# Joins of the first layer: whole-tile squares, single convolution taps, and x split tile by tile in the last output unit

## The reference

```python
# first block, l = 0 (conformer convolution), l = 1 (causal attention with forget gates)
for l in range(2):
    h = rmsnorm(x, g_mix[l])
    mem_k, mem_v = split(rmsnorm(mem, g_mem) @ w_mem_kv[l])        # mem: 256 tokens
    # l = 0: p = h @ w_in_a -> u (1536), q_mem (256)
    #        v = a * sigmoid(gate); v = causal_dwconv(v, width 31); v = silu(layernorm(v))
    x = x + concat([mix, memory_attention(q_mem, mem_k, mem_v)]) @ w_out[l]
    x = x + conv_ffn(rmsnorm(x, g_ffn[l]), ...)                    # up 2*2816, conv 3, silu*gate, down
x = rmsnorm(x, g_final)
# second block, 2 layers: rmsnorm, input projection, gated spatial mixing and GQA attention,
# output projection, x = x + rmsnorm(out, post_g)
```

## Time and profile before

| | us |
|---|---|
| median of 3 runs | 1788.6 (1787.67 to 1791.67) |
| the profiled execution, its own time | 1788.69 |
| its span | 1786.9 |
| PE busy in the span | 1685.6 (94%) |
| DVE / ACT / POOL busy | 886.1 / 739.2 / 721.1 |
| mean granted TensorE clock | 0.973 of full speed |
| DMA | 142.71 MB, mean 80 GB/s |

### The profile page before, as it was taken

One profiled execution on the slowest core, in us unless ns is written; L12 is line 12 of the kernel. 1 busy time (PEld: TensorE's weight loads), 2 busy tenths in 40 slices (PEclk: granted clock), 3 DMA queues, 4 the chain that ended last, 5 costly groups with the idle time before them and its releaser, 6 DMA issues.

```text
span 1786.9 us, 23856 instructions
## 1 busy us (share of the span) xinstructions
PE 1685.6 (94%) x8586; PEld 1292.2 (72%) x8586; DVE 886.1 (50%) x1360; ACT 739.2 (41%) x1143; POOL 721.1 (40%) x409
## 2 busy tenths in 40 slices
PE   5989899999999999999999999998999997899995
PEld 4756678888888776677788888886776676676674
DVE  7588745544420035434556666102655444655454
ACT  5333434444432245444455555222427443327350
POOL 4433343444444444443344444443334432334330
PEclk8999999999999999999999999998999998999997
DMA  5211133333333322112233333333211112211111
...
DMA packets 39819, 142.71 MB, mean 80 GB/s; under 512 B 4417, under 2 KB 4417, under 8 KB 39745
## 3 DMA queue, kind: packets, MB, share of 16 engines
...
## 4 chain that ended last, share of the span: by engine, by line
PE 82%; DVE 12%; ACT 3%; issue 2%; DMA 0%; POOL 0%; SPq 0%; DVEq 0%; ACTq 0%; POOLq 0%
PE banks L1469 23%; PE banks L1471 23%; PE banks L1470 23%; PE banks L1573 3%; PE banks L1608 3%; PE banks L1591 2%; DVE chain L1170 2%; DVE sq_sum L959 1%; PE banks L1664 1%; ACT prob L634 1%; PE banks L1541 1%; DVE pt L1456 1%; DVE xs_lo L1326 1%; PE banks L1847 1%; DVE nmax L1025 1%
## 5 line engine op out<-in xcount | busy, mean ns | idle before, releaser
L507 POOL TENSOR_TENSOR w_lo<-raw,w_hi 128x1024 fp32r<-128x1024 f32 x255 | 625.2, 2461 | 814.8 <-ACT w_hi L586 814.6
L1469 PE MATMUL banks<-xs_hi,w_hi 128*128 128x512 f32 x1592 | 649.0, 408 | 25.9 <-DVE xs_lo L1326 12.5
L1471 PE MATMUL banks<-xs_hi,w_lo 128*128 128x512 f32 x1592 | 627.3, 394 | 0.0
L1470 PE MATMUL banks<-xs_lo,w_hi 128*128 128x512 f32 x1592 | 626.7, 394 | 0.0
L586 ACT ACTIVATE w_hi<-raw 128x1024 fp32r<-128x1024 f32 x255 | 263.7, 1052 | 298.2 <-PE banks L1471 289.8
L1469 PEld LDWEIGHTS banks<-xs_hi,w_hi 128*128 128x128 f32 x1592 | 303.3, 191 | 109.3 <-issue 40.3
L1471 PEld LDWEIGHTS banks<-xs_hi,w_lo 128*128 128x128 f32 x1592 | 302.6, 190 | 65.8
L1470 PEld LDWEIGHTS banks<-xs_lo,w_hi 128*128 128x128 f32 x1592 | 303.8, 191 | 60.3 <-issue 2.9
L517 POOL TENSOR_SCALAR prob<-prob,rinv 128x512 f32<-128x512 f32 (+3 forms) x144 | 87.1, 619 | 183.6 <-DVE rinv L1034 183.5
L634 ACT ACTIVATE prob<-banks,nmax 128x512 f32<-128x512 f32 (+3 forms) x144 | 83.3, 583 | 169.6 <-DVE nmax L1025 169.4
L1471 PE MATMUL banks<-hid_hi,w_lo 128*128 128x512 f32 x352 | 139.1, 395 | 0.0
...
## 6 DMA issues: line engine op xcount, KB each, us to landing
...
out<-x SPq DMA_DIRECT2D x8, 256.0 KB, 2.0
...
sb_sb<-sbT ACTq DMA_DIRECT2D x2, 256.0 KB, 4.1
...
```

Source lines behind the costliest of these rows:

```text
L507: nc.gpsimd.tensor_tensor(w_lo[s][:].rearrange("p k c -> p (k c)"), raw[s][:], w_hi[s][:].rearrange("p k c -> p (k c)").bitcast(f32), SUB) ...
L1469: MM(dst, w_hi[slot][:, k, :], hi, start=start, stop=False)
L1470: MM(dst, w_hi[slot][:, k, :], lo, start=False, stop=False)
L1471: return MM(dst, w_lo[slot][:, k, :], hi, start=False, stop=stop)
```

## The change

It touches seven things.
1. **Start.** The squares of `memx` and x go into whole buffers `mem_sq` and `x_sq` (in the space of `glu` and `conv`, not yet used); DVE sums each with one `tensor_reduce`. ACT makes w_hi(1) behind the fourth tile of `mem_hi`, w_hi(2) before the squares of mem. The norm x has its `stat` in the second query unit and its `cast` in GLU unit 0; the two query units go to banks 2 and 3.
2. **Places.** The attention's steps move from slots 2, 7, ..., 47 to 12, 16, 21, ..., 55 (slot = 8j + k), `conv_parts` to behind units 6 to 10, `conv_fold` and `parts_down` by one unit, to 7 to 11.
3. **Taps.** DVE does one tap behind each k instead of two behind each attention step and the rest at the unit's end; `inverses` comes directly behind `maxima` and `even_down`. Of the last channel tile PE takes 24 taps and DVE 7.
4. **Layer norm.** The squares go into `glu`, no buffer has to be freed; `ln_stat` comes before the third unit of `U_MEM1`; the xs_lo of the memory tiles come behind the centring.
5. **invert.** `m` and `t` lie in the PSUM bank `b_mix`, and r alone in SBUF; no instruction has two inputs in SBUF.
6. **Last output unit.** x tiles 0 to 6 are split while PE runs unit 7 of the output projection, as it releases the tiles of xs (`xs_free`); DVE does xs_lo 0 to 5 before it adds the last unit, xs_lo 6 behind that, 7 behind the square.
7. **FFN down of layer 0.** Each tile of x is split behind its residual instead of all at the end.

```diff
-PE_TAPS = 16
-DVE_TAPS = CW - PE_TAPS
+PE_TAPS = (16, 16, 16, 16, 16, 24)
+DVE_TAPS = tuple(CW - n for n in PE_TAPS)
-A_AT = [divmod(2 + 5 * i, KT) for i in range(10)]
+A_AT = [divmod(12 + 43 * i // 9, KT) for i in range(10)]
...
-            def residual(first, name):
+            def residual(first, name, gain, change):
                 for m in range(KT):
                     high_for(first + m)
+                    if m == KT - 1:
+                        for k in range(KT - 1):
+                            tile_free(change, first + m, k)
+                            A(xs_hi[:, k, :], x[:, k, :], ACT.Copy, scale=col(gain, k)).then_inc(split_hi, 1)
                     act.wait_ge(acc_free, accs_before(first + m) + 1)
                     square(name, m, x[:, m, :])
+                A(xs_hi[:, KT - 1, :], x[:, KT - 1, :], ACT.Copy, scale=col(gain, KT - 1)).then_inc(split_hi, 1)
...
+                if k == 3:
+                    high(1)
-            high(1)
+            high(2)
             for k in range(KT):
-                if k >= 2:
-                    act.wait_ge(sq_added, norm_at["mem"][1] + k - 1)
-                A(sqm[k % 2][:], memx[:, k, :], ACT.Square).then_inc(squared, 1)
-            high(2)
+                A(mem_sq[:, k, :], memx[:, k, :], ACT.Square).then_inc(first_squared, 1)
             for k in range(KT):
                 if k % 2 == 0:
                     act.wait_ge(x_in[k // 2], 16)
                 A(xs_hi[:, k, :], x[:, k, :], ACT.Copy, scale=col("g_mix0", k)).then_inc(split_hi, 1)
-                square("x", k, x[:, k, :])
-                if k in (1, 4, 6):
-                    high(3 + (1, 4, 6).index(k))
+                A(x_sq[:, k, :], x[:, k, :], ACT.Square).then_inc(first_squared, 1)
+                if k == 1:
+                    high(3)
+            high(4)
+            high(5)
...
-                if t >= 2:
-                    act.wait_ge(ln_summed, t - 1)
-                A(sq[t % 2][:], conv[:, t, :], ACT.Square).then_inc(ln_squared, 1)
+                A(glu[:, t, 0:T], conv[:, t, :], ACT.Square).then_inc(ln_squared, 1)
...
-                m, r, t = small_m[:, 0:w], small[:, 0:w], small_t[:, 0:w]
+                m, t = (b_mix[:, TM + 64 * i:TM + 64 * i + w] for i in range(2))
+                r = small[:, 0:w]
...
-                    own.link(V.scalar_tensor_tensor(out=t, in0=r, scalar=-0.5, in1=r, op0=MUL, op1=MUL))
-                    own.link(V.tensor_tensor(t, t, m, MUL))
+                    own.link(V.tensor_tensor(t, m, r, MUL))
+                    own.link(V.scalar_tensor_tensor(out=t, in0=t, scalar=-0.5, in1=r, op0=MUL, op1=MUL))
...
-            def residual(first, name):
+            def residual(first, name, no, gain):
                 for m in range(KT):
                     u = first + m
+                    if m == KT - 1:
+                        for k in range(KT - 2):
+                            low(no, gain, k)
                     src = take_acc(u, accs_before(u))
                     V.tensor_tensor(x[:, m, :], x[:, m, :], src[:], ADD).then_inc(acc_free, 1)
+                    if m == KT - 1:
+                        low(no, gain, KT - 2)
                     add_square(name, m)
+                low(no, gain, KT - 1)
...
                     add_square(name, m)
+                    if l == 0:
+                        low(SP_Q, "g_mix1", m)
...
-                add_square("x", k)
-                if k == 3:
+                if k == 5:
                     invert("mem")
-                if k == 6:
-                    spread("mem", rstd_m, TM)
+            dve.wait_ge(first_squared, 2 * KT)
+            V.tensor_reduce(sq_sum[:], x_sq[:].rearrange("p k t -> p t k"), AX.X, ADD).then_inc(first_summed, 1)
+            spread("mem", rstd_m, TM)
...
                 for k in range(KT):
+                    at = KT * (j % 2) + k
                     for i in a_steps(j, k):
                         if i < att_m0.n:
                             maxima(att_m0, i)
-                        if t >= 0:
-                            conv_taps(t, at, at + 2)
-                            at += 2
+                        if 1 <= i <= att_m0.n:
+                            even_down(att_m0, i - 1)
                         if i < att_m0.n:
                             inverses(att_m0, i)
...
-                if t >= 0:
-                    conv_taps(t, at, DVE_TAPS if j % 2 else 8)
-                if 7 <= j < 11:
-                    conv_finish(j - 7)
+                    if t >= 0:
+                        conv_taps(t, at, at + 1)
+                if 8 <= j < 12:
+                    conv_finish(j - 8)
...
             glu_product(MT - 1)
+            own.wait()
+            conv_taps(MT - 1, 0, DVE_TAPS[MT - 1])
             conv_finish(MT - 2)
+            conv_finish(MT - 1)
+            layer_norm("ln", (0,), conv, MT, bank[2])
...
-            unit(U_QM0, U_QM0, first=KT * SP_A, before=[(2, lambda: stat("x"))], wait_acc=False)
-            unit(U_QM0 + 1, U_QM0 + 1, before=[(2, lambda: cast("x"))], wait_acc=False)
+            unit(U_QM0, U_QM0, first=KT * SP_A, wait_acc=False, dst=bank[2])
+            unit(U_QM0 + 1, U_QM0 + 1, before=[(2, lambda: stat("x"))], wait_acc=False, dst=bank[3])
...
+            ln_stat()
             mem_unit(U_MEM1 + 2, half_bank(acc[1], 0))
-            ln_stat()
+            cast("ln")
             mem_unit(U_MEM1 + 3, half_bank(acc[1], 1))
-            cast("ln")
```

152 lines of the change are left out of this document (71 added, 81 removed).

## The result

The changed kernel takes 1778.56 us (median of 4 runs, 1777.3 to 1781.08), the kernel before on the same chip 1789.74 (1787.67 to 1791.67): ratio 0.9938, 95% interval 0.9927 to 0.995, so 11.2 us faster. The forecast was 1767.0 and its range ended at 1778: the direction was right, half of the gain was missing, and the time lies just outside the range.

What follows compares the result with a forecast made beforehand. PE, busy 94% of the span, was taken to bound the kernel, with some 100 us idle at joins and DVE pacing the GLU stretch. From 1788.69, -4.0 - 5.4 - 0.4 - 4.6 - 1.1 - 6.2 = -21.7 gave 1767 us; range 1754 to 1778.

Steps and rivals of the forecast that it cites:

- Start: From the kernel's beginning to GLU unit 0: that unit begins at 43.5 instead of 55.8, 12.3 us earlier.
- My lower bound for the gain, 9: At the start: gain of only 9 us if the transfers or ACT hold up w_hi(2) and w_hi(4).
- GLU stage: GLU units, paced by DVE: product 0 to product 2 takes 48 to 49 us; only 4 of 12.3 + 2.5 arrive.
- Last tile and layer norm: Last convolution tile through layer norm to the projection's first tile: -3.9 - 0.6 - 0.9 = -5.4 us.
- net -0.6: Layer norm: statistics start at once, the next unit covers the inversion, PE idles 1.4 us before the first square; net -0.6.
- Last output units: Last output-projection unit, twice: PE's wait moves from the FFN's first tile to `stat`; gain 0.2 us each.
- Down stage: FFN down stage of layer 0: the 2.93 us wait and 1.7 of low clock go, -4.6 us.
- Inversion: Norm inversions: no instruction waits for POOL; -1.1 us in f1 and -6.2 in pre0 and pre1 together.
- The bound of 3.6 for writing PSUM: Inversion: at worst 0.1 us more per instruction, 1.2 in each of three exposed inversions, 3.6 in all; nothing was taken.
- The third rival: GLU stage eats the start's whole gain; unit 11 ends where it did or 3 us later, 1771 to 1775; chance 0.13.
- the forecast's own test of being wrong: Wrong if GLU unit 11 ends before 163 or after 173, or if `stat` of f0 is not waited for.

Runs made afterwards that it cites:

- b4: The changed kernel with the high split of weight unit 1 put behind all eight of memory's splits on ACT; 1779.08 us, ratio 0.9926.
- c3: The changed kernel with DVE's taps 2 to 5 of the convolution left out in tiles 0 to 4; 1771.14 us, ratio 0.9905.
- d2: c1 with PE doing 20 of the taps in tiles 0 to 2 instead of 16; 1764.78 us, ratio 0.9854.
- b3: The changed kernel with the order around the layer norm as in the kernel before; 1772.32 us, ratio 0.9897.
- d4: c1 with a tap put back between maxima and inverses, and b4's edit; 1761.94 us, ratio 0.9842.
- c1: The changed kernel with the edits of a3 and b3 together; 1764.1 us, ratio 0.9864.
- a3: The changed kernel with the next weights' high split on ACT put behind the last output unit's splits of x; 1768.49 us, ratio 0.9879.
- a2: The kernel before with only x split tile by tile in the FFN down stage of layer 0; 1783.78 us, ratio 0.9967.
- a1: The kernel before with only the inversion's m and t moved into the PSUM bank; 1780.79 us, ratio 0.9954.

## Why the forecast was right, and where it was wrong

The sum said -21.7 and the profile shows -7.6. In the order of the forecast's steps:

- **Start: mis-sized, 4.1 us.** (The forecast's own terms, 29.5 + 10.9 + 0.9 + 1.7, add up to 43.0 and not to 43.5, so by its working 4.6.) "The two reduces of DVE (I take 2.1 and 4.3 us, at the rate of its other instructions) lie beside PE" is the step that failed. They took 3.83 and 7.50, the longer ends at 40.8 and not near 31, and `stat` of x waits 2.35 us for it. The low clock behind it (3.4 us of it, 1.7 lost) is no more than the forecast had counted. Two things had to come together for the wait: the sum is 3.2 longer, and it begins at 33.37 instead of near 27, since VectorE's splits and the inversion of mem stand before it (the last two `xs_lo`, beside `w_lo`, take 3.70). Either by itself would have fitted before 38. The other 2 us lie ahead of that: the first query unit begins at 31.49 and not at 29.5, as ScalarE makes its `w_hi` from 27.94 on and not by 27.0, and PE waits 1.17 for GpSimd's part. One of them is of this execution: PE's first matmul comes at 10.00, in the kernel before at 8.98 and in most kernels below between 8.7 and 9.2. The strided sum of one input costs 1.83 ns per element (7.50 us for 4096), where an operation over 512 elements costs 0.69 us, 1.35 ns. My lower bound for the gain, 9, left this out. Beside it, the early split of weight unit 1 makes GpSimd hold `mem_lo` (four took 5.59); b4 prices that at 1.0.
- **GLU stage: the mechanism right, 2.3 short.** From product 0 to product 2 I said 48 to 49 us, and it is 48.6; that VectorE's taps bind there is shown by c3, with d2's exception. (12.3 and 2.5 off 73.74 would have been 58.9 for product 0, where the forecast has 59.7; 48.6 is met from there all the same.) Product 0 comes 1 us later behind GLU unit 0 than I took; I read this as ScalarE's exponential standing behind `mem_values_down(1)` (VectorE idle 3.79 at 61.90), which no run isolates. And `conv_parts(0)` to the last fold is 55.4 instead of 53.8.
- **Last tile and layer norm: the largest miss, 5.4 us.** The first half held: the sums are complete 19.0 us behind that unit's fold, where I had 19.4 (its terms add up to 19.2). The second half failed: "`ln_stat` starts at once and runs at its own 0.92 per tile" and "net -0.6". The 48 matmuls took 7.45, not 5.5, since the clock fell within them and stayed low through the whole third memory unit, 5.3 us instead of 2.9; then PE waits 1.50 for a bank that `mem_kv` frees only behind two norm tiles. b3 shows 2.1 of it to be the order; the rest goes with the length of the low stretch (in d4, where that is 3.6 us, the whole stretch is 17.0 where c1 has 20.0), and what sets that length is open. I had counted a low clock behind waits and none behind light work, though the earlier trace rows were followed by one before (205.2 to 208.9).
- **Last output units: right in place, 1.2 and 1.3 short.** `stat` is waited for, 2.18 and 2.23 us, where 2.7 was said; but the low clock behind it cost 3.2 and not 1.7. That is why the entry of f0 came out dearer than before instead of 0.2 cheaper. a3 confirms the chain and gives the remedy; that the same wait cost 0, 1.6 or 3.2 us of low clock in the traces of other kernels makes the size of this term, not its place, a matter of luck.
- **Down stage: right.** -4.6 said, -4.8 in the ledger, -5.5 alone (a2).
- **Inversion: right.** -1.1 and -6.2 said; the 1.10 at f1 are gone (and eaten by the wait at its `stat`), and from the `cast` of f1 to that of post1 it is -6.5, 5.4 of it between `stat` and `cast` of pre0 and pre1; 8.5 alone (a1). The bound of 3.6 for writing PSUM is refuted: 0.16 to 0.17 us for each instruction. One reason given for it was wrong though the number held: "with at most one input in SBUF none waits for POOL, as L979 did not". L981 and L982 of the kernel before have one input in SBUF each and took 2.38 and 2.30 us beside `w_lo`; what sets L979 apart is that its input lies in PSUM. The change helps those two because they now read PSUM as well. L991 to L993 keep one SBUF input and take 0.16 to 0.17 beside the same `w_lo`, so one SBUF input alone does not decide it. By the runs, a `TENSOR_SCALAR` and a `COPY` between SBUF buffers were held, a `TENSOR_TENSOR` or `SCALAR_TENSOR_TENSOR` with its other input in PSUM and a `TENSOR_REDUCE` were not; why is not shown.

The third rival (the GLU stage eats the gain of the start) came nearest, and the forecast's own test of being wrong did fire: GLU unit 11 ended after 173. But of the 14 us that the ledger lacks only 2.3 lie there; the rest is the start itself, the layer norm and the last output units. (By medians it is 11.6; the profiled execution was 2.5 us slower than the median.) The range failed since the start came out beyond its lower bound (9), and the layer norm and the output units, for which no bound was given, missed in the same direction. The last two have one cause in part in common: the clock was low for longer than the 1.7 us lost that the forecast had read behind a wait, 3.2 behind each wait at `stat`, and 5 in the layer norm against 3.5 before.
